# A two-block transformer on one core: order of the mixed tokens and of the last down-projection tiles in the FFNs of the second block

## The reference

```
x = layer_norm(alpha * x + 0.5 * swiglu(x, ffn_w_gu[l, 0], ffn_w_down[l, 0]), ...)
x = layer_norm(alpha * x + token_mixers(x, ...), ...)
x = layer_norm(alpha * x + 0.5 * swiglu(x, ffn_w_gu[l, 1], ffn_w_down[l, 1]), ...)
```

## Time and profile before

| | us |
|---|---|
| median of 3 runs | 3462.16 |
| lowest and highest | 3460.11 and 3462.34 |
| the profiled execution | 3459.79 |
| its span on the core | 3458.0 |
| TensorE busy in it | 3289.9 |

### The profile page before, as it was taken

The page is one execution under the profiler, slowest core; times in us unless marked ns, Lnnn a source line. Parts: engine busy times, 40 slices in busy tenths (PEclk is TensorE's granted clock), DMA queues, the critical chain, the costliest instruction groups (busy, mean ns, idle before and its releaser), DMA issues.

```text
span 3458.0 us, 54481 instructions
## 1 busy us (share of the span) xinstructions
PE 3289.9 (95%) x20208; PEld 2847.4 (82%) x20208; DVE 2273.9 (66%) x3250; ACT 1611.8 (47%) x2525; POOL 12.7 (0%) x13
## 2 busy tenths in 40 slices
PE   7999999999999998999899989997999999989996
PEld 6898888888788888999766689997999876679995
DVE  6573466537766537767686587677768667587686
ACT  5323344326544325435466454354445456654444
POOL 0000000000000000000000000000000000000000
PEclk9999999999999999999999999999999999999998
DMA  3200222222222222322111113222222211022322
GB/s 132 67 32 31 87 98 97 96 94 92 92 91 97 96 97 84 116 98 94 66 56 39 38 71 113 98 98 74 98 102 94 74 62 45 25 74 98 110 86 98
DMA packets 82907, 286.29 MB, mean 83 GB/s; under 512 B 9200, under 2 KB 11248, under 8 KB 82160
## 3 DMA queue, kind: packets, MB, share of 16 engines
q1 hardware_dynamic: 82528, 281.41, 23.6%
q0 software_dynamic: 144, 1.71, 0.1%
HBM read 280.98 MB, written 2.10 MB: 82 GB/s over the span
## 4 chain that ended last, share of the span: by engine, by line
PE 82%; DVE 10%; issue 4%; ACT 3%; DMA 1%; DVEq 0%; ACTq 0%; SPq 0%
PE gb L737 13%; PE gb L738 12%; PE gb L739 12%; PE gb L946 8%; PE gb L947 8%; PE gb L948 8%; PE pm L737 4%; PE pm L738 4%; PE pm L739 4%; PE gb L1504 2%; DVE wl L2401 1%; PE pm L1541 1%; PE pm L1521 1%; DVE rinv L2431 1%; DVE work_a L3253 1%
## 5 line engine op out<-in xcount | busy, mean ns | idle before, releaser
L737 PE MATMUL gb<-xh,wh 128*128 128x512 f32 (+1 forms) x1888 | 698.2, 370 | 59.7 <-DVE xl L2455 39.1
L738 PE MATMUL gb<-xl,wh 128*128 128x512 f32 (+1 forms) x1888 | 675.4, 358 | 0.0
L739 PE MATMUL gb<-xh,wl 128*128 128x512 f32 (+1 forms) x1888 | 674.9, 357 | 0.0
L2401 DVE TENSOR_TENSOR wl<-wst,wh 128x1024 fp32r<-128x1024 f32 (+2 forms) x392 | 440.2, 1142 | 264.9 <-ACT wh L1665 261.4
L1665 ACT CAST wh<-wst 128x1024 fp32r<-128x1024 f32 (+2 forms) x392 | 376.1, 980 | 452.3 <-DMA wst<-in_weights 452.1
L737 PEld LDWEIGHTS gb<-xh,wh 128*128 128x128 f32 x1888 | 369.4, 196 | 146.0 <-issue 61.9
L738 PEld LDWEIGHTS gb<-xl,wh 128*128 128x128 f32 x1888 | 370.1, 196 | 49.0 <-issue 4.8
L739 PEld LDWEIGHTS gb<-xh,wl 128*128 128x128 f32 x1888 | 369.3, 196 | 48.8
L946 PE MATMUL gb<-xh,hid 128*128 128x256 f32 x960 | 275.9, 287 | 20.8 <-DVE hid L2685 20.8
L947 PE MATMUL gb<-xl,hid 128*128 128x256 f32 x960 | 275.1, 287 | 0.0
L948 PE MATMUL gb<-xh,hid 128*128 128x256 f32 x960 | 275.0, 286 | 0.0
(11 more groups left out here) (458 smaller groups left out, 6489.4 us busy)
## 6 DMA issues: line engine op xcount, KB each, us to landing
wst<-in_weights SPq DMA_DIRECT2D x296, 512.0 KB, 3.3
work_a<-in_weights SPq DMA_DIRECT2D x160, 512.0 KB, 4.0
wst<-in_weights SPq DMA_DIRECT2D x62, 384.0 KB, 3.0
wst<-in_weights SPq DMA_DIRECT2D x28, 320.0 KB, 2.9
h<-in_x_t SPq DMA_DIRECT2D x2, 1024.0 KB, 6.2
out_t<-h SPq DMA_DIRECT2D x8, 256.0 KB, 2.2
tab<-in_first SPq DMA_DIRECT2D x1, 1984.0 KB, 15.0
tab<-in_second POOLq DMA_DIRECT2D x1, 1666.0 KB, 7.3
```

What stands on the lines that cost most here:

```text
L737: pe.matmul(dst, w_hi, x_hi, start=start, stop=False)
L738: pe.matmul(dst, w_hi, x_lo, start=False, stop=False)
L739: return pe.matmul(dst, w_lo, x_hi, start=False, stop=stop)
L2401: dve.tensor_tensor(wl[:, s, m, a], wst[:, s, m, a], f32(wh[:, s, m, a]), ALU.subtract).then_inc(lo_split, 1)
```

## The change

1. The start of a grouped FFN. VectorE makes T1, T2 and the low part of T1 first; then hidden tile 0, the sums and first splits of tile 2, T4, the low part of T2, `hid_low(0)`, `low_a22`, hidden tile 1, T3 and its low part, the low part of T4. ScalarE's order follows: it casts T1 and T2, then takes the Silu of tile 0 and the weights' high parts, and casts T3 only after hidden tile 1. TensorE's waits on these (`x_mix`) count in the new order. SyncE waits for two more splits ahead of its first block loads.
2. The end. In the last group tiles 4 to 7 are all made by token halves: `down_by_half(v, m)`, first half 0 of tiles 4, 5, 6, 7, then half 1 of them, with `first_mean` after the first of them and `sums` of half 0 between tiles 5 and 6 of half 1. The banks are new (`late_bank`), so that no half waits for a bank just written. VectorE and ScalarE do the additions, squares and sums of squares of tiles 4 and 5 by halves too. What is left of half 1 (squares of 4 and 5, tiles 6 and 7) moves to three places between the pairs of half 0 in `norm` (`late_group`), and ScalarE's squares of half 1 of tiles 6 and 7 after its pairs 1 and 3.
3. Names: the 2 in many index formulas becomes `PLAIN`, and three pairs of semaphores share one.

The core of the diff:

```diff
+        def late_bank(v, m):
+            return gb[:, 2 * m - 7, :] if m < 6 else pm[:, m - 6, :] if v else gb[:, 2 * m - 12, :]
...
-                    if j == 2 and p in ("P4", "P5", "P6", "P7"):
-                        pe.wait_ge(S("x_mix"), 2 * MIXES * part_run + MIXES + {"P5": 1, "P6": 2, "P7": 3, "P4": 5}[p])
+                    if j == PLAIN and p in ("P4", "P5", "P6", "P7"):
+                        pe.wait_ge(S("x_mix"), 2 * MIXES * part_run + MIXES + {"P5": -2, "P6": 1, "P7": 3, "P4": 5}[p])
...
+                def down_by_half(v, m):
                     a, b = GROUPS[2]
+                    c, s, q, t = c0 + down_chunk(2) + m // 2, m // 2 % 2, m % 2, HV[v]
+                    if v == 0:
+                        if m >= 6:
+                            pe.wait_ge(h_ready, 6 * (n - 1) + m - 3)
+                        wait_half(c, q)
+                    elif m < 6:
+                        pe.wait_ge(S("h_half"), 5 * part_run + m - 3)
+                    else:
+                        pe.wait_ge(h_ready, 6 * (n - 1) + m - 5)
+                    for k in range(b - a):
+                        col = slice(k * P, k * P + P)
+                        mm = three(late_bank(v, m)[:, t], wh[:, s, q, col], wl[:, s, q, col], hid[:, 0, k, t], hid[:, 1, k, t],
+                                   k == 0, k == b - a - 1)
+                    mm.then_inc(S("down_half") if v == 0 else chunk_done if q else half_done, 1)
...
-                    for m in range(2, KT - (r == 2)):
+                    for m in range(2, KT if r < 2 else SHIFT):
                         down(r, m)
-                down_last()
+                for v in range(2):
+                    for m in range(SHIFT, KT):
+                        down_by_half(v, m)
+                        if m == SHIFT and v == 0:
+                            first_mean(n)
+                        elif m == SHIFT + 1 and v == 1:
+                            sums(n, l, 0, S("h_half"), 5 * part_run + 3)
...
-                for t in range(3):
+                for t in range(2):
                     act.wait_ge(S("x_mix"), 2 * MIXES * part_run + t + 1)
                     act.copy(mixed_x(t + 1, 0), mixed_raw(t + 1)).then_inc(up_lin, 1)
                 gate_out(0)
+                high_a(PLAIN)
+                high_v(0, PLAIN)
                 hid_high(0)
-                high_a(2)
-                high_v(0, 2)
-                high_v(1, 2)
-                high_a22(2)
+                high_v(1, PLAIN)
+                high_a22(PLAIN)
                 gate_out(1)
                 hid_high(1)
+                act.wait_ge(S("x_mix"), 2 * MIXES * part_run + 7)
+                act.copy(mixed_x(3, 0), mixed_raw(3)).then_inc(up_lin, 1)
...
-                for t in range(1, 5):
-                    mixed(t)
-                dve.wait_ge(S("x_mix"), 2 * MIXES * part_run + MIXES)
-                for t in range(1, 4):
-                    mixed_low(t)
+                mixed(1)
+                mixed(2)
+                mixed_low(1)
                 plain_product(0)
+                sum_v31(PLAIN)
+                sum_v2_v4(PLAIN)
+                low_a(PLAIN)
+                low_v(0, PLAIN)
+                mixed(4)
+                dve.wait_ge(S("x_mix"), 2 * MIXES * part_run + 5)
+                mixed_low(2)
                 hid_low(0)
-                sum_v31(2)
-                sum_v2_v4(2)
-                low_a(2)
-                low_v(0, 2)
-                low_a22(2)
+                low_a22(PLAIN)
                 plain_product(1)
                 hid_low(1)
+                mixed(3)
+                mixed_low(3)
...
+                d, down_at = c0 + down_chunk(2), 2 + 4 * part_run
+                for m in (4, 5):
+                    dve.wait_ge(S("down_half"), down_at + m - 3)
+                    dve.wait_ge(S("h_shifted"), 4 * (n - 5) + m - SHIFT + 1)
+                    dve.tensor_tensor(h[:, m, LO_TOKENS], late_bank(0, m)[:, LO_TOKENS], h[:, m, LO_TOKENS], ALU.add).then_inc(S("h_half"), 1)
+                for k in range(SHIFT):
+                    dve.tensor_tensor(h[:, k, :], h[:, k, :], mu[:, :], ALU.subtract).then_inc(xc_ready, 1)
...
+            def late_group(c0, n, l):
+
+                d = c0 + down_chunk(2)
+
+                def squares():
+                    late_square(n, 4)
+                    late_square(n, 5)
+
+                def sixth():
+                    dve.wait_ge(half_done, d + 4)
+                    tail_residual(n, 6, 1, late_bank(1, 6), l)
+
+                def seventh():
+                    tail_add(n, 1)
+                    dve.wait_ge(chunk_done, d + 4)
+                    tail_residual(n, 7, 1, late_bank(1, 7), l)
+
+                return {0: squares, 1: sixth, 2: seventh}
...
-                norm(n, l, late=(lambda: late_down(c0, n, l, FS_C),), first=(c0 + FS_C, 0), split=next_split(c0 + FS_C + 1))
+                norm(n, l, late_in=late_group(c0, n, l), first=(c0 + FS_C, 0), split=next_split(c0 + FS_C + 1))
```

More of the change, by code:

```diff
@@ L49 @@
 BLK = KT // 2 * P
-UNITS = [range(max(a_, 2), b_) for a_, b_ in GROUPS]
+PLAIN = 2
+UNITS = [range(max(a_, PLAIN), b_) for a_, b_ in GROUPS]
 N_UNITS = sum(len(u_) for u_ in UNITS)
@@ L1706, in norm_root, with norm @@
                     act.activation(rt[:, t], rt[:, t], ACT.Sqrt, bias=eps_of[EPS_LN]).then_inc(rt_ready, 1)
-            def norm(n, ln=None, gain=None, final=False, k_ln=None, late=None, late_at=2, first=None, split=None):
+            def norm(n, ln=None, gain=None, final=False, k_ln=None, late=None, late_at=2, first=None, split=None, late_in={}):
                 def high(j, v):
@@ L2385, in _ @@
                 grouped_ffn(c0, g0, 0, n, l)
-                norm(n, l, k_ln=0, late=lambda: tail_square(n, 7, 1), first=(c0 + FS_C, 0), split=next_split(c0 + FS_C + 1))
+                norm(n, l, k_ln=0, late_in={1: lambda: tail_square(n, 6, 1), 3: lambda: tail_square(n, 7, 1)}, first=(c0 + FS_C, 0), split=next_split(c0 + FS_C + 1))
                 mixer2(l, c0 + FS_C, n + 1, 2 + l)
@@ L2389, in _ @@
                 grouped_ffn(c0 + FS_C + M2_C, g0 + FF_G + M2_G, 1, n + 2, l)
-                norm(n + 2, l, k_ln=2, late=lambda: tail_square(n + 2, 7, 1), late_at=0, first=(c0 + LAYER_C, 0), split=next_split(c0 + LAYER_C + 1))
+                norm(n + 2, l, k_ln=2, late_in={1: lambda: tail_square(n + 2, 6, 1), 3: lambda: tail_square(n + 2, 7, 1)}, first=(c0 + LAYER_C, 0), split=next_split(c0 + LAYER_C + 1))
         @block.vector
@@ L2406, in split_lo, with norm @@
                     split_half(c, s, m, cols[m])
-            def norm(n, ln=None, final=False, gain=None, late=None, late_at=1, first=None, split=None):
+            def norm(n, ln=None, final=False, gain=None, late=None, late_at=1, first=None, split=None, late_in={}):
                 in_h = final or ln is not None
@@ L2476, in half @@
                             late[0]()
+                        if v == 0 and j in late_in:
+                            late_in[j]()
                 variance(0)
@@ L3407, in _ @@
                 grouped_ffn(c0 + FS_C + M2_C, g0 + FF_G + M2_G, 1, n + 2, l)
-                norm(n + 2, l, late=(lambda: late_down(c0 + FS_C + M2_C, n + 2, l, FS_C),), late_at=0, first=(c0 + LAYER_C, 0), split=next_split(c0 + LAYER_C + 1))
+                norm(n + 2, l, late_in=late_group(c0 + FS_C + M2_C, n + 2, l), first=(c0 + LAYER_C, 0), split=next_split(c0 + LAYER_C + 1))
 def layout(inputs):
```

163 lines of the change are left out of this document (90 added, 73 removed).

## The result

| | before | after |
|---|---|---|
| median, us (11 runs each) | 3460.5 (3457.3 to 3463.38) | 3470.1 (3468.0 to 3474.4) |
| ratio to before, 95% interval | | 1.003 (1.0021 to 1.0039) |
| the profiled execution, us | 3459.8 | 3474.0 |
| its span, us | 3458.0 | 3472.0 |

The change costs 9.6 us, 0.3%. The forecast was +4.4 with a range up to 3477: the sign and the range held, the size was short by 5 us, and the time lies just beyond what I had called the same.

A forecast was written before the change was run, and what follows sets the result against it. TensorE was busy for 95% of the span, with FFN starts set by VectorE's chain. Starts +14.5 and ends -10.1 gave +4.4 us: 3464.2 against the profiled execution, 3466.6 against the median; range 3451 to 3477.

The forecast's parts named there:

- The bound: At a grouped FFN's start, the length of VectorE's chain sets P1(3), not when P1(2) began.
- rival (b): FFN start: the earlier P1(2) counts in full, -4.3 us per start, total 3435 us; chance 0.11.
- The new wait: TensorE's P6(2) would wait some 8 us for `low_v(1, 2)` in each of the four FFN starts.
- The start, +14.5: Reordered starts of the four FFNs: 3.2 + 3.8 + 4.3 + 3.2 us lost, bounds +9 to +19.
- The forecast of nothing for SyncE's new waits: FFN start: SyncE's added waits are on splits of chunks long done and cost nothing.
- The second term, the clock: FFN start: TensorE's lower clock after its wait costs P6(2) and P3(2) 1.9 us, in front of P1(3).
- The extras of the second and third FFN: Start: Silu 0.6 us later in the second FFN; first chunk and blocks' DMA about 1.1 later in the third.
- The end, -10.1: FFN ends by halves with the norms behind: 2 x -2.5 + 2 x -2.55 us, bounds -14 to 0.
- Rival (c): FFN end: VectorE's tail is late for `sums`, so the second part brings nothing; +18 us, 3480; chance 0.15.
- The cause of the give-back: Norm: four more half-tile VectorE instructions and ScalarE's square of tile 6 waiting for a late sum; 0.9 or 0.85 us each.
- the case near 3482: FFN ends: by the skill's rule, half tiles cost 19 us instead of 3.7; chance 1 in 100.
- Rival (a): Whole change: the clock mostly stays up and the parts cancel or better, 10.9 - 12 = -1 us, 3461; chance 0.18.

The follow-up runs named there:

- Kernels 3 and 5: 3: after with the FFN start in the order TensorE needs, 3455.0 us; 5: 3 with ScalarE's cast of T3 behind the copy P3(2) needs, 3445.1 us.
- kernel 1: Before with only the new FFN start (orders of VectorE, ScalarE and TensorE), the old end and without SyncE's two new waits: 3476.5 us, ratio 1.0052 to before.
- kernel 2: After with the FFN start of before, so the new ends alone: 3453.1 us, ratio 0.9983 to before.
- kernel 4: After with 15 unused matmuls on a constant ahead of P6(2), to keep TensorE busy through its wait: 3468.3 us, ratio 1.0029 to before.
- Kernel 6: The new ends with the old FFN start, plus ScalarE's square of tile 6 moved in the norm from behind pair 1 to behind pair 2: 3447.8 us.

## Why the prediction was right or wrong

**The bound.** Right. P1(3) is set by VectorE's chain, and P1(2) 3.5 us earlier was worth nothing (rival (b), 3435, refuted). Kernels 3 and 5 are the positive proof: the same instructions in an order that brings `low_v(1, 2)` and `low_a(3)` forward give 14.5 and 24 us against after.

**The new wait.** Right in place and about in size: four waits for `low_v(1, 2)`, "some 8 us", measured 8.3 at the longest, 31.6 together.

**The start, +14.5.** Mis-sized; measured +19.9. That is just beyond its upper bound of +19; by the ratios of the times it is +18.0 (kernel 1) or +16.3 (after against kernel 2), inside the bounds. The forecast's two terms can be held against the traces. P6(2) was to come 2.3 us after the T+20.7 of the chain, with 0.6 and 1.1 more in two FFNs: 10.9 in all. It came at T+23.81, 24.54, 24.35 and 24.71: 14.6. The missing 3.7 is the step "the product 5.49 to 6.18, the block sums to 8.76": I took the sums to follow at once. They don't, for two reasons. The product is followed by VectorE's wait for its own end, and the first sum starts 0.43 later than I had it even where no block is late: kernel 1 has P6(2) at T+23.43 and not at 23.0, 1.7 over the four. (Its four P6(2) are 10.9 behind T+20.7, the forecast's own number, but by luck: it has these 1.7 and neither of the two extras.) And I did not ask when the sums' own operand lands. The chain of waits of after has their DMA in it (start us, us, what), and VectorE's timeline of before has the same sums at T+10.4:

```profile
1332.70 5.04 DMA work_a<-in_weights
```

```profile
1343.03 1.22 DVE L2666 TENSOR_TENSOR wst<-work_a 128x1024 f32<-128x1024 f32 x1
```

The blocks land at 1337.74, T+6.7, and VectorE stands still until then for 0.70, 0.80, 0.91 and 1.60 us in the four FFNs, 4.0 together. Some 1.3 of it are the wait for its own product, which kernel 1 has too (0.31 to 0.34 each); the late blocks cost 2.7. Before, the mixing of all four tokens hid the landing (T+3.3 to 6.5 against T+10.4); the change took that cover away. In kernel 1 the same cover was gone and the blocks, at T+3.3 to 6.5, were still in time. So it takes both: the earlier sums, and a later transfer, which comes in the kernels that have SyncE's two waits and the new end. The 1.7 and the 2.7, less the 0.7 by which the extras below fell short, are the 3.7. The forecast of nothing for SyncE's new waits is thus not confirmed. I had asked the question of the Silu, and not of the transfer. The second term, the clock, was 0.9 per FFN beyond VectorE's own T+26.85, 3.6; measured, by kernel 4, 4.7. The extras of the second and third FFN, forecast as 0.6 and 1.1 from the Silu, were 0.63 and 0.34 there (VectorE's first product at T+6.15 and 5.86, against 5.52), and the fourth had one of its own, from its DMA. About 0.6 more comes between P1(3) and the first mean.

**The end, -10.1.** Right in the profiles, -9.5. The time of kernel 2 says less, -5.9 with an interval from -2.8 to -9.0, so -10.1 is more than the times bear out; its profile has -7.9. How the miss of 5 us on the sum divides between the start and the end therefore depends on which is believed: by the profiles it is the start's alone. S' 3.4 us earlier was measured as 3.42. The low parts of the second, third and fourth pair came 0.79, 1.74 and 1.50 later against S (forecast 0.8, 1.7 and 1.5). After the first FFNs the norm gave back 1.6 and 1.2 (0.9 forecast), after the second 0.6 and 0.8 (0.85 forecast). The wait for the first pair is 1.14 ("about 1.4"), the next are 2.80 and 0.29 (forecast 1.5 to 3; only one was). The second `sums` was to come at S+18.7 to 19.4 and came at S+19.77 and S+18.66. Rival (c), VectorE's tail late for `sums`, didn't come: no wait stands in front of 1672.68. Behind the second FFN one step was told wrongly with the right sum: the first product of the second `sums` starts 2.7 us later against S and not 6, but then waits 2.00 for the squares, so that the next stage's products start at S+21.4, as worked out.

```profile
2380.25 1.22 PE L830 MATMUL pm<-h,com 128*128 128x256 f32 x2 [4.81 <-DVE h L2536]
2383.47 1.22 PE L832 MATMUL pm<-sq,com 128*128 128x256 f32 x2 [2.00 <-DVE sq L2529]
```

**The cause of the give-back.** The prediction named ScalarE's square of tile 6 and VectorE's added half-tile instructions. Kernel 6 shows the square's share: moving it brings the fourth low part 0.71 us earlier in each norm and takes back 1.5 us after the two second FFNs; up to 3.0 of the 5.8 us that the four norms of kernel 2 gave away, if the first FFNs are counted as they stand. The rest was not taken apart.

**The halves.** The prediction held 0.120 us per product of 256 tokens against the rule of the Trainium skill (TensorE: Matmul & The Clock Gate, "Why this matters for your kernels"). In after the first half tile takes 1657.43 - 1654.56 = 2.87 us for 24 products, 0.12 each: the case near 3482 is out.

**Rival (a).** The clock was to stay up through the start. It did not: 0.50 from P6(2) to P1(3) in the first FFN. In the norm it was right for the first pair and wrong behind the wait of 2.80, as two windows of after show:

```profile
1672.68:1681.89 9.21, 8.07 (x61) 7.61 (x59) 7.48 (x11) 5.67 (x11) 0.00 (x0) 1.00 0.37 121
```

```profile
1685.60:1692.40 6.80, 6.45 (x30) 6.16 (x31) 5.05 (x9) 5.84 (x10) 0.00 (x0) 0.54 0.01 2
```

## What to carry to other kernels

When work is moved off the front of an engine that is already full, follow the whole chain to the consumer that really ends last, and of each instruction that moves up ask when each of its operands lands, transfers too: what was hidden behind the old order turns up as idle time in the new one. A wait that is added ahead of a transfer belongs to the same question. An order by first use is good only over all users: T3, used last, was still ahead of the splits needed first, and putting those first won 14.5 us where the change had lost 10. An instruction of half a microsecond that frees a bank, or a cast that others wait for, must not be queued behind one that waits for another engine; two such moves were worth 10 us and, less surely, 3.

## What was unexpected of the hardware

At the lower clock the first 12 products behind a wait took 2.73 us (P6(2) of after, 1354.83 to P3(2) at 1357.56) and the next 12 took 2.56 (to P1(3) at 1360.12), 0.213 each. The 0.228 per product that I read from P1(2) in the trace of before was the mean of such a first group, with its late start in it. The Trainium skill (TensorE: Matmul & The Clock Gate, "Back-to-back issue gap") gives the number of columns over 1.2 GHz for this level, by which 256 columns take 0.213 us, an estimate from that page: the second group agrees. At the full level the same section has 256 columns over 2.4 GHz and 2.5 ns, 0.109 us; the trace has 0.12.

The granted clock also differed between executions where nothing had been changed: in the mixer of the first layer it was 0.50 for 6.8 us in the profiled execution of after, at a place where it was 1.00 in that of before, behind the same 1.8 us wait. The mixer took 3.2 us longer. Over all kernels the same mixer took 329.8 to 334.4 us, in step with the time at 0.50.
